# A merged stage of a hybrid encoder layer: backward chunks in two slots and forward chunks in four, in place of one and five

## The chip, the cores and the metric

The kernel runs on one core of one Trainium2 chip, in a single launch. The metric is the device time in microseconds, the median of several runs; less is better. PE is the matmul engine TensorE, DVE is VectorE, ACT is ScalarE, POOL is GpSimd, and SP (SyncE) issues transfers.

## The reference

One encoder layer over two sequences, of 1024 and 2048 tokens (24 chunks of 128 tokens in all), in float32:

```python
h = rms_norm(x, norm_in)
proj = h @ w_in                    # 1024 -> q, k, v, z_attn, z_ssd, xbc, dt_f, dt_b
y_ssd = ssd_branch(...)            # conv, forward and backward chunked scans, gate, norm
y_attn = dilated_mixture(rotary(q), rotary(k), v) * silu(z_attn)
x = x + concat([y_ssd, y_attn]) @ w_out
y = rms_norm(x, norm_f)

def ssd_scan(x, dt_raw, b_mat, c_mat, a_log, dt_bias):   # chunks of 128, 16 heads
    ...
    y_diag = jnp.einsum('bclsge,bcsgep->bclgep', cb[..., None] * lmat, xc)
    states = jnp.einsum('bcsgn,bcsgep->bcgepn', bc, decay_to_end[..., None] * xc)
    # carried from chunk to chunk: carry * chunk_decay + states
    y_off = jnp.einsum('bclgn,bcgepn->bclgep', cc, states_in) * jnp.exp(acum)[..., None]
    return (y_diag + y_off).reshape(bsz, s_len, h, p)
```

The backward scan is the same function on the flipped sequence, so its states are carried from the last chunk of a sequence to the first.

## The kernel before

The kernel runs in phases: a front phase (norm, the first projections, the convolution), two short phases that prepare the decays, the merged stage `late_phase`, the attention, and the output projection. The change touches `late_phase` alone.

`late_phase` does two things side by side. The first is the projection of q, k and za (the attention gate): 144 units from `late_units()`, ordered by turn (three blocks of 1024 tokens), name (q, k, za: 16 units each), pair of weight tiles, half of the block, and ab. A unit is 24 matmuls of 128x128 by 128x512 (L1067): float32 is split into a high and a low part, so that the products are h_hi by w_hi, h_hi by w_lo, h_lo by w_hi, eight of each. The unit's number n is also its slot; u = n % 2 is its output buffer. The second is the scan: for 24 chunks first the backward states (`add_back` on PE, `back_step` on DVE, `weigh` on POOL, `store_back` and `load_back` on SP), and then for 24 chunks the forward pass.

Every engine walks over the slots in the same loop, `for slot, unit in enumerate(units)`: PE does `scan(slot)` and then `multiply(unit)`; DVE does `scan(slot)` and then `rotate(unit)`, if the unit is q or k; ACT does its part of the scan and then `take(unit)`, if the unit is za. The engines are tied together by semaphores, and each engine works strictly in its own order. Slots 0 to 23 carry one backward chunk each (`first_forward = NT`, 24). From slot 24 on a forward chunk has `CYCLE` = 5 slots, its parts:

- part 0: PE computes the diagonal of the chunk before (`diagonal(n - 1)`, 16 heads, L1133) and the first quarter of the decays (`decays`, L1088); DVE `gated(n - 1)` and `choose(n, 0)`; POOL `scale_x` (L907) and `keep_state` (L897); ACT copies the decays and does `norm(n - 1)`.
- part 1: decays, products of B and C (L1100), the forward state's part (`state_part(n, 0)`, L1116); DVE choose, finish, skip_part, state_part.
- part 2: decays, `add_state` (L1124); DVE choose, next_state; POOL `skip_x`.
- part 3: decays, add_state, `state_part(n, 1)`; DVE choose, next_state, state_part; ACT the exponentials (L1191).
- part 4: nothing of the scan on PE; DVE `whole_m(n)` (L1298), which multiplies the 16 decay matrices by C times B; POOL `add_rest(n)` (L922, L925), SP `load_rows(n + 1)` and `load_states(n + 1)`.

`diagonal(n)` waits for `whole_m(n)` (semaphore f_m_steps), for both state parts and for x. `gated(n)` waits for the diagonal and for `add_rest(n)`.

`rotate(unit)` waits for the unit's own products (l_out). For u = 0 it is two instructions (L1240, product with the table). For u = 1 it is two products (L1245) and two additions (L1249, both inputs in SBUF), which turn the pair of units into the rotated rows.

POOL also splits the weights: `split(w)`, two pieces of L871, L874 and a DMA issue (L858), in each slot with slot % 4 = 0 and in each with slot % 4 = 3. It waits there for the last products that use the buffer. The order of POOL's queue in the loop is:

```python
if part == 0: scale_x(n); keep_state(n)
if slot % 4 == 0: split(slot // 2 + 2)
if part == 2: skip_x(n)
if slot % 4 == 3: split(slot // 4 * 2 + 3)
if part == 4: add_rest(n)
```

At the end of a turn ACT loads the next block of h in halves (`load_h`, 2048 KB for h_hi and for h_lo of each half). The first half is issued in the slot after its last use, slots 46 and 94, behind what ACT has of the scan in that slot. `multiply` waits for it at the first unit of the next turn, slots 48 and 96.

Of the kernel before, what the change touches and what calls it, by code (L numbers as in the profile page):

```python
# [32 lines left out]
NT = sum(TILES)  # L33
# [729 lines left out]
    return units  # L763


CYCLE = 5


def late_phase(nc, sem, c, params, scratch, t_in, st, h_hi, h_lo):
# [3 lines left out]

    quads = HEADS // 4
    units = late_units()
    first_forward = NT
    second = TILES[0]
    turned_over = TILES[1]
    weights = len(units) // 2
# [7 lines left out]
    with ExitStack() as stack:  # L787
# [43 lines left out]
        def state_ready(j):  # L831

            return j + 1 + (j >= turned_over)

        def part_of(slot):

# [5 lines left out]
        def _(pool):  # L842
# [87 lines left out]
                split(w)  # L930
            weigh(0)
            for slot in range(len(units)):
                if slot + 1 < first_forward:
                    weigh(slot + 1)
                n, part = part_of(slot)
                if part == 0:
                    scale_x(n)
                    keep_state(n)
                if slot % 4 == 0:
                    split(slot // 2 + 2)  # L940
                if part == 2:
                    skip_x(n)
                if slot % 4 == 3:
                    split(slot // 4 * 2 + 3)
                if part == 4:
                    add_rest(n)

        @block.sync
        def _(sp):
            def load_back(j):  # L950
                if j >= 2:

                    sp.wait_ge(sem["b_added"], j - 1)
                sp.dma_start(xb[:, j % 2, :], by_chunk["xb"][NT - 1 - j, :, :]).then_inc(sem["b_in"][j % 2], 16)

            def store_back(j):
                sp.wait_ge(sem["b_state"], state_ready(j))
                sp.dma_start(scratch["states"][NT - 1 - j, :, :], state[:, j % 2, :]).then_inc(sem["b_stored"][j % 2], 16)

            def load_rows(n):  # L960
                if n:

                    sp.wait_ge(sem["f_seg"], quads * n)
                else:
                    sp.wait_ge(sem["f_rows_set"], 6)
                sums = scratch["sums"].rearrange("(d q h) (c l) -> c d q h l", d=DIR, q=2, l=P)
                for d in range(DIR):
                    at = 64 * d + 2 * HEADS
                    sp.dma_start(rows[at:at + 2, :, :].bitcast(F32), sums[n, d, :, :, :]).then_inc(sem["f_rows_in"], 16)
                sp.dma_start(shift[:, :].bitcast(F32), scratch["shift"][:, n * P:(n + 1) * P]  # L970
                             ).then_inc(sem["f_rows_in"], 16)

            def load_x(n):

                if n < 2:
                    sp.wait_ge(sem["b_added"], NT)
                else:
                    sp.wait_ge(sem["f_diag"], n - 1)
                    sp.wait_ge(sem["f_scaled"], 2 * n - 2)
                sp.dma_start(xb[:, n % 2, :], by_chunk["xb"][n, :, :]).then_inc(sem["f_in"][n % 2], 16)  # L980

            def load_states(n):
                if n:

                    sp.wait_ge(sem["f_off"], 2 * n)
                    sp.wait_ge(sem["f_cb"], n)
                else:
                    for u in range(2):
                        sp.wait_ge(sem["b_stored"][u], 16 * (NT // 2))
                sp.dma_start(bc[:, :, :], scratch["bct"].rearrange("(g n) t -> n g t", n=NST)[:, :, n * P:(n + 1) * P]  # L990
                             ).then_inc(sem["f_states_in"], 16)
                sp.dma_start(s_back[:, :], scratch["states"][n, :, :]).then_inc(sem["f_states_in"], 16)

            def load_gate(n):
                if n:

                    sp.wait_ge(sem["f_out"], n)
                sp.dma_start(gate[:, :], by_chunk["zs"][n, :, :]).then_inc(sem["f_gate_in"], 16)

            def store_y(n):  # L1000
                sp.wait_ge(sem["f_out"], n + 1)
                sp.dma_start(by_chunk["y_ssd"][n, :, :], spare[:, :]).then_inc(sem["f_stored"], 16)

            def store(unit):
                u = unit.u
                sp.wait_ge(sem["l_staged"][u], unit.n // 2 + 1)
                first = unit.b * BLOCK + unit.half * CW
                sp.dma_start(scratch[unit.name][unit.row:unit.row + P, first:first + CW], stage[:, u, :]
                             ).then_inc(sem["l_stored"][u], 16)

            load_back(0)
            load_back(1)
            sp.dma_start(table[:, :, :], t_in["rope"][:, :, BLOCK:]).then_inc(sem["l_rope_in"], 16)
            sp.dma_start(gain[:, :], params["norm_ssd"].to_broadcast([P, D_SSD])).then_inc(sem["f_consts"], 16)
            sp.dma_start(skip[:, :], params["d_skip"].to_broadcast([P, HEADS])).then_inc(sem["f_consts"], 16)
            for slot, unit in enumerate(units):
                if slot < first_forward:
                    store_back(slot)
                    if slot == first_forward - 4:
                        load_rows(0)  # L1020
                        load_gate(0)
                    if slot == first_forward - 1:
                        load_x(0)
                        load_x(1)
                        load_states(0)
                n, part = part_of(slot)
                if part == 1 and n:
                    store_y(n - 1)
                    load_gate(n)
                if part == 4 and n + 1 < NT:  # L1030
                    load_rows(n + 1)
                    load_states(n + 1)
                if part == 1 and 2 <= n + 1 < NT:
                    load_x(n + 1)
                if unit.turn == 1 and unit.name == "q" and unit.n == first_of_half[1, 0]:

                    sp.wait_ge(sem["l_taken"][1], unit.ropes_before // 2)
                    sp.dma_start(table[:, :, :], t_in["rope"][:, :, 0:BLOCK]).then_inc(sem["l_rope_in"], 16)
                if slot + 2 < first_forward:
                    load_back(slot + 2)  # L1040
                if slot:
                    store(units[slot - 1])
            store(units[-1])
            store_y(NT - 1)
            for u in range(2):
                sp.wait_ge(sem["l_stored"][u], 16 * (len(units) // 2))
            sp.wait_ge(sem["f_stored"], 16 * NT)

        @block.tensor
        def _(pe):  # L1050
# [84 lines left out]
                last.then_inc(sem["f_diag"], 1)  # L1135

            def scan(slot):
                if slot < first_forward:
                    add_back(slot)
                n, part = part_of(slot)  # L1140
                if part == 0:
                    if n:
                        diagonal(n - 1)
                    decays(n, 0)
                elif part == 1:
                    decays(n, 1)
                    products(n)
                    state_part(n, 0)
                elif part == 2:
                    decays(n, 2)  # L1150
                    add_state(n, 0)
                elif part == 3:
                    decays(n, 3)
                    add_state(n, 1)
                    state_part(n, 1)
# [73 lines left out]
        def _(dve):  # L1229
# [108 lines left out]
                                               ALU.mult, ALU.mult).then_inc(sem["f_out"], 1)  # L1338

            def scan(slot):  # L1340
                if slot < first_forward:
                    back_step(slot)
                n, part = part_of(slot)
                if part == 0:
                    if n:
# [8 lines left out]
                elif part == 1:  # L1354
                    choose(n, 1)
                    if n:
                        finish(n - 1)
                    skip_part(n)
                    state_part(n, 0)
                elif part == 2:  # L1360
                    choose(n, 2)
                    next_state(n, 0)
                elif part == 3:
                    choose(n, 3)
                    next_state(n, 1)
                    state_part(n, 1)
                elif part == 4:
                    whole_m(n)

            dve.wait_ge(sem["f_consts"], 32)  # L1370
            nc.vector.memset(state[:, 0, :], 0.0).then_inc(sem["b_state"], 1)
            for slot, unit in enumerate(units):
                scan(slot)
                if unit.rope:
                    if unit.turn < 2 and unit.n == first_of_half[unit.turn, 0]:
                        dve.wait_ge(sem["l_rope_in"], 16 * (unit.turn + 1))
                    rotate(unit)
            gated(NT - 1)
            finish(NT - 1)

# [839 lines left out]
```

## Time and profile before

| what | value |
|---|---|
| median of 3 runs | 3931.37 us (3925.37 to 3935.82) |
| the profiled execution | 3925.94 us |
| its span, first to last instruction | 3924.3 us |
| mean granted TensorE clock | 0.957 of full speed |
| PE busy | 3614.0 us (92%) |
| PE weight loads busy | 2850.7 us (73%) |
| DVE busy | 2146.7 us (55%) |
| POOL busy | 1594.6 us (41%) |
| ACT busy | 1360.7 us (35%) |
| POOL's two additions of add_rest, L922 and L925, mean of each | 2.38 and 2.43 us |
| DMA | 521.87 MB, mean 133 GB/s |

Busy times are shares of the whole span, over phases that have different limits. A row of the timeline is a run of equal instructions: when it started, how long it lasted from the first start to the last end, and in brackets how long the engine was idle before it and what released it. "issue" as the releaser says that the profile shows nothing that the engine waited for. The granted clock (PEclk) is 1.00 at 2.4 GHz and 0.50 at 1.2 GHz. Ends of matmuls are modelled; the starts are what periods are taken from.

### The profile page before, as it was taken

How to read it: one execution, taken by the hardware profiler on the slowest of the kernel's cores; microseconds unless marked ns; L12 is line 12 of the kernel's file. 1: busy time of each engine (PE TensorE's matmuls, PEld its weight loads, DVE VectorE, ACT ScalarE, POOL GpSimd, SP SyncE). 2: the span in 40 equal slices, each digit the busy share in tenths (PEclk: the TensorE clock that was granted, in tenths of full speed). 3: DMA queues.
4: the chain of work that ended last, by engine and by line, in shares of the span. 5: the costliest groups of instructions: out<-in, count | busy, mean ns of one | idle time of the engine just before them, and what ended most of it. 6: DMA issues, size and time to landing. Idle time of an engine off the chain costs nothing. (4 is left out here: it accounts for less than half of the span.)

```text
span 3924.3 us, 57718 instructions
## 1 busy us (share of the span) xinstructions
PE 3614.0 (92%) x20917; PEld 2850.7 (73%) x20917; DVE 2146.7 (55%) x4515; ACT 1360.7 (35%) x3566; POOL 1594.6 (41%) x1471
## 2 busy tenths in 40 slices
PE   6899999998875999899989998999999997899998
PEld 5777777887753667677767776677777775788887
DVE  2262145206414664366436653788888887465554
ACT  2122112212110003212322123778778885222222
POOL 5336342453505666567666664424233332100000
PEclk9999999999987999999999999999999998999999
DMA  4424422422314654634453342745544544444443
GB/s 166 150 77 138 170 77 72 136 94 64 102 40 160 212 166 137 209 122 136 128 185 120 122 142 89 172 125 136 137 127 114 139 132 128 162 158 154 166 152 103
DMA packets 366864, 521.87 MB, mean 133 GB/s; under 512 B 27595, under 2 KB 257555, under 8 KB 363859
## 3 DMA queue, kind: packets, MB, share of 16 engines
q1 hardware_dynamic: 329683, 402.80, 32.6%
q0 software_dynamic: 27456, 94.78, 8.1%
q10 hardware_dynamic: 9472, 20.97, 1.5%
q8 instruction: 152, 2.49, 0.3%
q14 instruction: 101, 0.83, 0.1%
HBM read 334.18 MB, written 184.29 MB: 132 GB/s over the span
## 5 line engine op out<-in xcount | busy, mean ns | idle before, releaser
L1713 ACT ACTIVATE attn_p_sb<-attn_p_sb,attn_o_sb 128x256 f32<-128x256 f32 (+1 forms) x1152 | 535.0, 466 | 183.7 <-DVE attn_o_sb L1747 178.2
L235 POOL TENSOR_TENSOR front_w_hi<-front_w_raw,one 128x1024 fp32r<-128x1024 f32 (+1 forms) x96 | 165.9, 1728 | 566.0 <-PE front_out L432 532.2
L1747 DVE CUSTOM_DVE_ANT_0 attn_p_sb<-attn_s_ps,attn_mask 128x256 f32<-128x256 f32 (+1 forms) x1152 | 368.8, 376 | 43.9 <-PE attn_s_ps L1646 43.7
L1067 PE MATMUL late_out<-h_hi,late_w_hi 128*128 128x512 f32 x1152 | 344.5, 443 | 22.5 <-issue 22.5
L1537 POOL COPY attn_q_apart<-attn_q 128x128 f32<-128x128 f32 (+2 forms) x256 | 136.9, 535 | 523.9 <-PE attn_s_ps L1646 517.5
L1067 PEld LDWEIGHTS late_out<-h_hi,late_w_hi 128*128 128x128 f32 x1152 | 225.0, 197 | 119.6 <-issue 78.4
L369 DVE TENSOR_SCALAR front_acc<-front_chan,front_consts 128x1024 f32<-128x1024 f32 (+2 forms) x36 | 38.8, 1077 | 473.3 <-ACT front_chan L281 473.3
L1186 ACT COPY late_m<-late_seg 128x512 f32<-128x512 f32 x96 | 55.9, 583 | 680.4 <-PE late_seg L1088 671.1
L1067 PE MATMUL late_out<-h_hi,late_w_lo 128*128 128x512 f32 x1152 | 286.7, 391 | 0.0
L1067 PE MATMUL late_out<-h_lo,late_w_hi 128*128 128x512 f32 x1152 | 284.5, 389 | 0.0
L1659 PE MATMUL attn_pt_ps<-ident,attn_p_sb 128*128 128x128 f32 x1920 | 278.4, 282 | 0.4 <-ACT attn_p_sb L1713 0.4
L1674 PE MATMUL attn_ot_ps<-attn_pt_sb,attn_v 128*64 128x128 f32 x3840 | 273.2, 280 | 0.0
L1659 PEld LDWEIGHTS attn_pt_ps<-ident,attn_p_sb 128*128 128x128 f32 x1920 | 203.9, 141 | 82.4 <-ACT attn_p_sb L1713 59.3
L375 DVE SCALAR_TENSOR_TENSOR front_acc<-front_chan,front_consts,front_acc 128x1024 f32<-128x1024 f32 (+2 forms) x144 | 258.4, 1795 | 5.1
L1067 PEld LDWEIGHTS late_out<-h_hi,late_w_lo 128*128 128x128 f32 x1152 | 218.4, 190 | 47.0
L432 PE MATMUL front_out<-front_w_hi,h_hi 128*128 128x512 f32 x768 | 203.9, 407 | 51.3 <-POOL front_w_lo L238 35.1
L1067 PEld LDWEIGHTS late_out<-h_lo,late_w_hi 128*128 128x128 f32 x1152 | 216.2, 188 | 45.0
L871 POOL TENSOR_TENSOR late_w_hi<-late_w_raw,one 128x512 fp32r<-128x512 f32 x144 | 152.4, 1058 | 220.1 <-PE late_out L1067 200.5
L1674 PEld LDWEIGHTS attn_ot_ps<-attn_pt_sb,attn_v 128*64 128x64 f32 x3840 | 203.7, 136 | 48.0 <-issue 48.0
L238 POOL TENSOR_TENSOR front_w_lo<-front_w_raw,front_w_hi 128x1024 fp32r<-128x1024 f32 (+1 forms) x96 | 230.1, 2397 | 7.5
L1713 ACT ACTIVATION_READ_ACCUMULATOR attn_p_sb<-attn_p_sb,attn_o_sb 128x1 f32 x1152 | 217.0, 188 | 0.0
L432 PEld LDWEIGHTS front_out<-front_w_hi,h_hi 128*128 128x128 f32 x768 | 147.1, 196 | 86.2 <-POOL front_w_lo L238 39.8
(211 smaller groups left out, 7380.1 us busy)
## 6 DMA issues: line engine op xcount, KB each, us to landing
front_w_raw<-w_in POOLq DMA_DIRECT2D x84, 512.0 KB, 4.1
output_parts<-s_o SPq DMA_DIRECT2D x24, 1584.0 KB, 6.5
late_w_raw<-w_in POOLq DMA_DIRECT2D x144, 256.0 KB, 3.9
s_o<-attn_o_sb SPq DMA_DIRECT2D x128, 264.0 KB, 3.0
late_xb<-s_xb SPq DMA_DIRECT2D x48, 640.0 KB, 5.8
s_zs<-front_stage SPq DMA_DIRECT2D x48, 256.0 KB, 2.0
s_v<-front_stage SPq DMA_DIRECT2D x48, 256.0 KB, 2.2
s_states<-late_state SPq DMA_DIRECT2D x24, 512.0 KB, 3.3
```

What stands on the lines that cost most here:

```text
L235: nc.gpsimd.tensor_tensor(hi, raw, one.to_broadcast([P, 2, cols]), ALU.mult).then_inc(sem["w_split"], 1)
L238: nc.gpsimd.tensor_tensor(lo, raw, hi.bitcast(F32), ALU.subtract).then_inc(sem["w_split"], 1)
L375: nc.vector.scalar_tensor_tensor(a, chan[:, k:k + conv.tokens], consts[:, at:at + 1], a, ALU.mult, ALU.add).then_inc(sem["tap_done" if k < ...
L432: last = nc.tensor.matmul(out[u][:, :], lhs, rhs, start=first, stop=h is h_lo and k == KT - 1)
L871: nc.gpsimd.tensor_tensor(w_hi[w % 3][:, k, :], w_raw[:, piece, :, :], one.to_broadcast([P, KT // 2, P]), ALU.mult).then_inc(sem["l_w_step ...
L1067: last = nc.tensor.matmul(out[u][:, :], w[s][:, k, :], h[:, k, half], start=first, stop=h is h_lo and k == KT - 1)
L1186: nc.scalar.copy(m[:, 4 * q:4 * q + 4, :].rearrange("p h l -> p (h l)"), seg[0][:, :]).then_inc(sem["f_decay"], 1)
L1537: nc.gpsimd.tensor_copy(dst[:, r * n:(r + 1) * n], src[:, at]).then_inc(sem["a_apart"][p - 1], 1)
L1659: last = nc.tensor.transpose(pt_ps[g % 2][:, h, k, :], p_sb[g % 4][:, h, k * P:(k + 1) * P], c["ident"][:, :])
L1674: last = nc.tensor.matmul(ot_ps[cut, g % 2, :], v[step.p][:, pattern.value_chunk(step.i, k), cut], pt_sb[g % 4][:, h, k, :], start=k == 0, ...
L1713: last = nc.scalar.activation(cut, cut, ACT.Exp, scale=-1.0, bias=o_sb[g // 4 % ring][:, g % 4, h, VW:OW], accum_out=o_sb[g // 4 % ring][: ...
L1747: last = nc.vector.tensor_tensor_reduce(out=p_sb[g % 4][:, h, 0:width], in0=s_ps[g % 2][h][:, 0:width], in1=mask[:, step.pattern.strip(ste ...
```

## The change

The backward pass takes 48 slots, a chunk in each even one. A forward chunk takes four slots, so that the forward pass begins at slot 48 and ends with slot 143 as before. What was in part 4 moves to part 3: `add_rest` on POOL, `load_rows` and `load_states` on SP, and `whole_m` on DVE, where it stands behind `rotate` of the same slot.

```diff
-CYCLE = 5
+CYCLE = 4
...
-    first_forward = NT
+    first_forward = 2 * NT
...
+        def chunk_back(slot):
+
+            return slot // 2 if slot < first_forward and slot % 2 == 0 else None
+
...  (POOL)
-                if slot + 1 < first_forward:
-                    weigh(slot + 1)
+                j = chunk_back(slot)
+                if j is not None and j + 1 < NT:
+                    weigh(j + 1)
...
-                if part == 4:
+                if part == 3:
                     add_rest(n)
...  (SP)
+                j = chunk_back(slot)
                 if slot < first_forward:
-                    store_back(slot)
+                    if j is not None:
+                        store_back(j)
...
-                if part == 4 and n + 1 < NT:
+                if part == 3 and n + 1 < NT:
                     load_rows(n + 1)
                     load_states(n + 1)
...
-                if slot + 2 < first_forward:
-                    load_back(slot + 2)
+                if j is not None and j + 2 < NT:
+                    load_back(j + 2)
...  (PE)
-                if slot < first_forward:
-                    add_back(slot)
+                if chunk_back(slot) is not None:
+                    add_back(chunk_back(slot))
...  (DVE)
-                if slot < first_forward:
-                    back_step(slot)
+                if chunk_back(slot) is not None:
+                    back_step(chunk_back(slot))
...
-                elif part == 4:
-                    whole_m(n)
...
                     rotate(unit)
+                n, part = part_of(slot)
+                if part == 3:
+                    whole_m(n)
```

## Rows read from the trace of the kernel before

**Rows 1.** The page, part 1: busy time, share of the span and instructions.

```profile
PE 3614.0 (92%) x20917; PEld 2850.7 (73%) x20917; DVE 2146.7 (55%) x4515; ACT 1360.7 (35%) x3566; POOL 1594.6 (41%) x1471
```

**Rows 2.** Busy time by stretch, with granted clock, DMA share, GB/s.

```profile
1230.27:1424.08 193.81, 181.12 (x673) 128.63 (x674) 131.08 (x116) 0.00 (x0) 132.49 (x96) 0.96 0.64 207
1424.08:2433.57 1009.49, 963.28 (x4195) 725.82 (x4195) 533.16 (x627) 264.45 (x337) 631.21 (x466) 0.96 0.42 139
```

**Rows 3.** Timeline of PE, backward slots 3, 4 and 5 (their first rows).

```profile
1253.81 1.88 PE L1076 MATMUL late_work<-late_scaled,late_xb 128*128 128x512 f32 x4
...
1261.01 1.88 PE L1076 MATMUL late_work<-late_scaled,late_xb 128*128 128x512 f32 x4
...
1270.89 3.06 PE L1076 MATMUL late_work<-late_scaled,late_xb 128*128 128x512 f32 x4 [2.51 <-DVE late_state L1262]
```

**Rows 4.** Timeline of PE, first rows of slots 54 to 59 (chunk 6, then diagonal).

```profile
1674.97 3.68 PE L1133 MATMUL late_work<-late_xb,late_m 128*128 128x64 f32 x32
...
1684.67 0.50 PE L1088 MATMUL late_seg<-late_rows,late_shift 64*128 64x512 f32 x2
...
1692.92 0.50 PE L1088 MATMUL late_seg<-late_rows,late_shift 64*128 64x512 f32 x2
...
1699.86 0.50 PE L1088 MATMUL late_seg<-late_rows,late_shift 64*128 64x512 f32 x2
...
1708.44 1.98 PE L1067 MATMUL late_out<-h_hi,late_w_hi 128*128 128x512 f32 x8
...
1716.44 4.96 PE L1133 MATMUL late_work<-late_xb,late_m 128*128 128x64 f32 x32 [2.40 <-issue]
```

**Rows 5.** Timeline of chunk 2, whose units are za: DVE and PE, slots 37 to 39.

```profile
1534.86 2.35 DVE L1298 TENSOR_TENSOR late_m<-late_m,late_cb_ps 128x1024 f32<-128x1024 f32 x2
...
1538.98 1.98 PE L1067 MATMUL late_out<-h_hi,late_w_hi 128*128 128x512 f32 x8
...
1544.42 3.68 PE L1133 MATMUL late_work<-late_xb,late_m 128*128 128x64 f32 x32
```

**Rows 6.** Timeline of PE and the DMA issues of ACT at the two h loads.

```profile
1627.89 3.75 PE L1067 MATMUL late_out<-h_hi,late_w_hi 128*128 128x512 f32 x8 [10.31 <-issue]
...
2013.82 0.53 ACTq L1173 DMA_DIRECT2D h_hi<-s_h  x1
...
2036.39 3.56 PE L1067 MATMUL late_out<-h_hi,late_w_hi 128*128 128x512 f32 x8 [12.14 <-issue]
```

**Rows 7.** Waits, 1430 to 2440 us: in total, times, longest us.

```profile
PE late_work L1133 <- issue: 18.1, 8, 2.4
```

**Rows 8.** Timeline of DVE and POOL behind the part 3 products of chunk 6.

```profile
1708.64 1.29 DVE L1245 TENSOR_TENSOR late_stage<-late_out,late_table 128x512 f32<-128x512 f32 x2 [4.24 <-PE late_out L1067]
...
1709.31 1.91 POOL L907 TENSOR_TENSOR late_scaled<-late_xb,st_weight 128x1024 f32<-128x1024 f32 x1
...
1709.96 4.11 DVE L1249 TENSOR_TENSOR late_stage<-late_a_turned,late_stage 128x512 f32<-128x512 f32 x2
...
1714.00 2.34 DVE L1298 TENSOR_TENSOR late_m<-late_m,late_cb_ps 128x1024 f32<-128x1024 f32 x2
```

**Rows 9.** Timeline of DVE, whole_m of chunk 5, whose part 3 is even.

```profile
1670.93 2.34 DVE L1298 TENSOR_TENSOR late_m<-late_m,late_cb_ps 128x1024 f32<-128x1024 f32 x2
```

**Rows 10.** Timeline of DVE, the longest pair of L1249, slot 64.

```profile
1760.14 6.04 DVE L1249 TENSOR_TENSOR late_stage<-late_a_turned,late_stage 128x512 f32<-128x512 f32 x2
```

**Rows 11.** Timeline of POOL, the split of slot 27 (1445.40), first and last row.

```profile
1445.55 1.04 POOL L871 TENSOR_TENSOR late_w_hi<-late_w_raw,one 128x512 fp32r<-128x512 f32 x1 [5.60 <-PE late_out L1067]
...
1451.77 0.79 POOL L858 DMA_DIRECT2D late_w_raw<-w_in  x1 [0.29 <-DMA late_w_raw<-w_in]
```

**Rows 12.** Busy time and granted clock in the diagonal of slot 99.

```profile
2060.11:2067.10 6.99, 6.99 (x33) 6.87 (x34) 1.09 (x2) 0.00 (x0) 3.98 (x5) 0.50 0.57 187
```

**Rows 13.** Timeline of PE, first rows of slots 99 and 100.

```profile
2060.11 7.06 PE L1133 MATMUL late_work<-late_xb,late_m 128*128 128x64 f32 x32 [2.40 <-issue]
...
2074.64 0.50 PE L1088 MATMUL late_seg<-late_rows,late_shift 64*128 64x512 f32 x2
```

## The prediction

> **What bounds the kernel now.** I read the page first: TensorE (PE) is busy 92% of the span [rows 1]. Then the stretches. The merged stage runs from the first backward product at 1230.27 to the last projection product at 2433.57, 1203.3 us: 193.81 us for the 24 slots that carry the backward chunks, 1009.49 us for the 120 slots of the forward chunks [rows 2]. PE works almost without a break in both, and the change gives it the same matmuls in another order. So I price only what PE loses: each slot's period, from its first matmul to the next slot's, against the shortest period of its kind.
>
> PE's rows in order of time give these shortest periods. A slot with a backward chunk takes 7.20 us (1253.81 to 1261.01) [rows 3]. Of a forward chunk, part 0 (the diagonal of the chunk before, then decays) takes 9.70, part 1 8.25, part 2 6.94, part 3 8.58 [rows 4], and part 4, which carries the projection alone, 5.44 (1538.98 to 1544.42) [rows 5]. A chunk is 38.91. Chunk 0 has no diagonal ahead of it, 3.61 us less.
>
> - Backward: 193.8 - 24 x 7.2 = 21 us lost. Every fourth slot ends with PE waiting 2.5 us for VectorE's state update (1261.01 to 1270.89 is 9.88, not 7.20) [rows 3]: five such waits at 2.7 are 13.4 us, and the slow restarts after some of them about 5. The other 2 are the start of the stage and stay.
> - Forward: 1009.5 - (24 x 38.9 - 3.6) = 79 us lost. 26 of it lies at the two places where h is replaced: PE idles 10.31 and 12.14 us, and the restarts run slow (8 matmuls in 3.75 and 3.56 us) [rows 6]. The other 53 lie around eight waits of the diagonal, L1133, 18.1 us of gap in all [rows 7], their slow restarts, and a few waits of 0.5 to 1.4 us for a late choose.
>
> **What the eight waits are.** The diagonal needs whole_m (L1298). At the end of chunk 6, part 3 has an odd slot, so `rotate` of that slot has four instructions, and they wait for its products, which end at 1708.44. VectorE then runs L1245 (1708.64), the pair L1249 from 1709.96 for 4.11 us, and only then whole_m, 1714.00 to 1716.34 [rows 8]. The diagonal starts at 1716.44, 8.0 us after the products of part 3; part 4 covers 5.44 of them [rows 4]. In the chunk before, part 3 is an even slot: whole_m runs 1670.93 to 1673.27 and the diagonal at 1674.97 does not wait [rows 9]. Where the units are gates (za) VectorE has no rotate: whole_m ends at 1537.2, 1.8 us before the end of the part 3 products at 1538.98 [rows 5].
>
> **The change part by part.**
>
> 1. Backward chunk in two slots (48 slots, 24 with a chunk). Per two slots PE has 7.2 + 5.4 = 12.6 us, and VectorE one state step and one pair of rotates instead of two steps. I take the waits for the state as gone: 21 - 2 = -19 us. POOL's weigh is half as frequent too. If the cover failed it would be the 2.5 us wait again, so at most 0.
>
> 2. The forward waits go in their old form: -53 us. They belong to a pattern (whole_m in part 4, odd and even slots in turn) that is no longer there; what comes in its place is the next point.
>
> 3. Part 4 removed, whole_m after `rotate` of part 3. Forward chunks now start at slot 48, so part 3 is slot 51 + 4n: always odd, u = 1. The diagonal is the first thing that PE does in the next slot. No slot lies between, so the whole distance "end of the part 3 products to end of whole_m" becomes idle time of PE. It applies where the part 3 slot is q or k: slots 48 to 79 and 96 to 127, 16 chunks. For the 8 chunks in za slots it costs 0 by [rows 5] (cover 1.8 us).
>  - Size of the wait. L1245 begins 0.2 after the products; the pair L1249 begins 1.5 after them. How long the pair takes is the unknown: at least 1.29 us, what the pair L1245 of the same shape takes, 4.11 beside POOL's L907 [rows 8], 6.04 at worst [rows 10]. Which one? The split of a weight runs in slots 4k+3, which is now always part 3: from 1445.55 to 1452.56, 7.0 us [rows 11], beginning with the slot. add_rest (L922 and L925, 2.4 each by the table of the profile) is behind it: it runs 7.2 to 12.0 us after the start of part 3, and the products end at 8.58. So when the pair comes, at 10.1, POOL is in L925, then in L907. Let the first half of the pair wait for the end of L925 (12.0, done 12.7) and the second for L907 (14.4, done 15.0): 4.9 us. With whole_m at 2.34 the diagonal starts 17.4 after the start of part 3, a wait of 8.8. Bounds: 0.2 + 1.3 + 1.3 + 2.3 + 0.1 = 5.2, and with the pair at 6.04, 9.9.
>  - Clock. After PE's wait of 2.4 us at 2060.11 the granted clock is 0.50 for the 6.99 us of the diagonal (1.2 of 2.4 GHz), and the slot lasts 2074.64 - 2060.11 = 14.53 instead of 9.70: 4.8 us [rows 12, 13]. The new wait is over three times as long, so I take this, the dearest common case. Low bound: the restart at 1627.89 without a diagonal, 16 matmuls in 6.7 us instead of 4.0, 2.7 us [rows 6]. High bound, an estimate: the slow stretch of [rows 12] and the same again on all of the projection products, 6.
>  - Behind the waiting diagonal in PE's queue stand the decays of the next chunk and the products of part 0; nothing passes it, so the time is lost. VectorE's gated and choose of part 0 come later by the same amount as PE's part 1, which needs them, and POOL's scale_x and keep_state run meanwhile: no second wait.
>  - 16 x (8.8 + 4.8) = +218 us.
>
>  The pair's 4.9 us rests on the two engines excluding each other. In the trace the first L1249 of [rows 8] stands beside L907 and takes 4.11 us where L1245's pair takes 1.29. The Trainium skill, SBUF — State Buffer, "Who interferes with whom", says that a VectorE instruction with two SBUF inputs contends with a GpSimd instruction that reads SBUF, the later one blocking fully. By that rule the pair is 4.9 and the wait 8.8; without it 1.29 and 5.2. The trace agrees in size.
>
> 4. Replacing h. The first replacement now has slots 46 and 47 as backward slots in front of it, 7.2 + 5.4 + 0.4 of cover instead of 6.94 + 8.58: +2.5. At the second, slots 94 and 95 become parts 2 and 3, and slot 96 begins with a diagonal. The load was issued at 2013.82 in ScalarE's queue, 9 us into the slot, behind norm [rows 6]; in part 2 it has no norm in front of it and goes out about 8 us earlier. Landing some 25 us after, against 19.6 of cover: about -6. Together -4. SyncE's waits move with their parts: load_rows and load_states now stand in part 3, where f_off is released 2.7 us into the slot, and the next q store behind them has to wait for a rotate anyway. The rows are needed after the diagonal, more than 12 us later. 0.
>
> Sum: -19 - 53 + 218 - 4 = +142 us. The profiled execution took 3925.9 (span 3924.3 and 1.6 around it): 4068. The median of the runs is 5.4 above it, so 4073.
>
> **The rivals.**
>
> - A, the pair is short (POOL has passed by): 16 x (5.2 + 4.8) = 160, total +84, 4015. Against: POOL's split starts with part 3 by its own wait, so add_rest meets the pair in each chunk.
> - B, the clock costs less. The restart at 2036.39, dense projection products, lost 3.56 - 2.40 = 1.2 us [rows 6], the one at 1627.89 2.7. With 2.7: 16 x 11.5 = 184, +108, 4039. Against: each restart here begins with the diagonal of 64-column products, as in [rows 12, 13]. The Trainium skill, TensorE: Matmul & The Clock Gate, "What's actually happening", sees the ramp penalty below 1% of a typical span. That is 39 us; the sum would be 16 x 8.8 + 39 - 76 = +104, 4035. The trace speaks against it where PE waits at each chunk.
> - C, dearer: pair at 6.04 and the clock at 6 us: 16 x 15.9 = 254, +178, 4109; the same if za chunks begin to wait because ScalarE's exp comes 2 us later.
> - D, faster: whole_m ends within the products of part 3, as in [rows 9], for q and k too. Then nothing is added: -76, 3855. It decides below 76 / 16 = 4.8 us lost per chunk. The lower bound of the wait alone is 5.2, as rotate cannot start before the products end and stands in front. Only if VectorE's order were other than I read it.
>
> **How the numbers follow.** Forecast 0.60, A 0.12, B 0.14, C 0.11, D 0.03. The time is that of the forecast, 4073. The range 4012 to 4110 reaches from A to C. All cases but D are slower by far over 0.3% (12 us, about what a measurement of this kernel can tell from no change): slower 0.96, faster 0.03, same 0.01.
>
> **What would show it.** In the changed kernel's trace: L1133 with 16 gaps of about 9 us put down to "issue", none in za slots; a granted clock near 0.5 behind each; L1249 at 4 to 6 us in slots 4k+3 with POOL's L925 and L907 beside it; no wait for L1262 in the backward slots. The stage would last some 1345 us. Wrong would be: waits at za chunks, gaps of 5 us, or a diagonal at full clock.

## The result and the profile after

The changed kernel took 4074.9 us (median of 4 runs, 4074.4 to 4076.3) against 3929.0 us before (3925.4 to 3935.8): a ratio of 1.0367, 95% interval 1.0354 to 1.0379. It is 146 us slower. The forecast was 4073.

In the changed kernel the line numbers have moved: L1083 is the backward product (before L1076), L1074 the projection (L1067), L1140 the diagonal (L1133), L1252 and L1256 the two pairs of rotate (L1245, L1249), L1305 whole_m (L1298), L926, L929, L911, L901 POOL's add_rest, scale_x and keep_state (L922, L925, L907, L897), L1180 the load of h (L1173).

Busy time by stretch, backward slots and then forward slots (engines in the order PE, PEld, DVE, ACT, POOL, then granted clock, DMA share, GB/s). It answers to [rows 2]:

```profile
1230.75:1536.19 305.44, 305.44 (x1248) 234.97 (x1248) 170.03 (x145) 10.25 (x16) 204.11 (x166) 0.99 0.57 181
1536.19:2580.78 1044.59, 896.12 (x3620) 672.10 (x3619) 491.00 (x598) 247.68 (x315) 552.66 (x396) 0.86 0.37 120
```

PE is busy for all of the backward stretch, at a mean granted clock of 0.99. In the forward stretch it is busy for 896 of 1045 us, and the mean granted clock fell from 0.96 to 0.86. The stage lasts 1350.0 us against 1203.3.

The timeline of PE in two backward slots and the one after, which answers to [rows 3]:

```profile
1257.88 1.88 PE L1083 MATMUL late_work<-late_scaled,late_xb 128*128 128x512 f32 x4
...
1265.09 1.98 PE L1074 MATMUL late_out<-h_hi,late_w_hi 128*128 128x512 f32 x8
...
1270.53 1.88 PE L1083 MATMUL late_work<-late_scaled,late_xb 128*128 128x512 f32 x4
```

A slot with a chunk takes 7.21 us and one without 5.44, and no slot ends in a wait for the state: the 21 us above the shortest periods shrank to 2.1, nearly all of it in the first slot.

The waits of the forward stretch (total us, times, longest), which answer to [rows 7]:

```profile
PE late_work L1140 <- issue: 133.1, 16, 8.5
```

One of the 16, at slot 76. The timeline of PE, beside [rows 4, 13]:

```profile
1857.11 0.50 PE L1095 MATMUL late_seg<-late_rows,late_shift 64*128 64x512 f32 x2
...
1863.87 1.97 PE L1074 MATMUL late_out<-h_lo,late_w_hi 128*128 128x512 f32 x8
1874.31 7.06 PE L1140 MATMUL late_work<-late_xb,late_m 128*128 128x64 f32 x32 [8.46 <-issue]
1881.30 0.80 PE L1095 MATMUL late_seg<-late_rows,late_shift 64*128 64x512 f32 x2
...
1889.65 0.50 PE L1095 MATMUL late_seg<-late_rows,late_shift 64*128 64x512 f32 x2
```

Part 3 lasts 1874.31 - 1857.11 = 17.20 us instead of 8.58, and the next part 0 15.34 instead of 9.70. What VectorE and POOL do meanwhile, in their timelines, beside [rows 8]:

```profile
1865.88 1.29 DVE L1252 TENSOR_TENSOR late_stage<-late_out,late_table 128x512 f32<-128x512 f32 x2 [4.24 <-PE late_out L1074]
1867.21 4.74 DVE L1256 TENSOR_TENSOR late_stage<-late_a_turned,late_stage 128x512 f32<-128x512 f32 x2
1871.87 2.34 DVE L1305 TENSOR_TENSOR late_m<-late_m,late_cb_ps 128x1024 f32<-128x1024 f32 x2
...
1866.75 2.34 POOL L929 TENSOR_TENSOR late_y<-late_y,late_spare 128x1024 f32<-128x1024 f32 x1
1869.05 2.35 POOL L911 TENSOR_TENSOR late_scaled<-late_xb,st_weight 128x1024 f32<-128x1024 f32 x1
```

The chain reads without a gap: products end (1865.70, the start of the slot plus the shortest period of a part 3, 8.58), L1252, the pair L1256, whole_m to 1874.21, the diagonal at 1874.31. The first of the pair stands behind L929 and the second behind L911, which is what the prediction laid out. VectorE had been idle for 4.24 us ahead of L1252.

The clock in the same place, busy time by stretch (the wait, the diagonal, decays and the first eight products, the rest of the slot), beside [rows 12]:

```profile
1865.70:1874.31 8.61, 0.15 (x2) 0.03 (x1) 8.29 (x6) 0.00 (x0) 8.53 (x5) 0.70 0.20 77
1874.31:1881.30 6.99, 6.99 (x32) 6.87 (x32) 0.00 (x0) 0.00 (x0) 5.56 (x6) 0.50 0.14 38
1881.30:1885.60 4.30, 4.30 (x11) 3.10 (x11) 3.09 (x3) 2.17 (x4) 0.00 (x0) 0.50 0.23 61
1885.60:1889.65 4.05, 4.05 (x17) 3.07 (x15) 0.00 (x0) 2.63 (x4) 0.00 (x0) 0.92 0.02 4
```

The clock is 1.2 GHz for all of the diagonal, for the decays and for the first third of the products behind it. In none of the 16 slots does PE have a gap behind the start of the diagonal, so what such a slot loses is lost to the clock alone. For comparison the 4.30 us behind the diagonal of [rows 12], in the kernel before:

```profile
2067.10:2071.40 4.30, 4.30 (x14) 3.17 (x14) 3.09 (x3) 2.18 (x4) 0.00 (x0) 0.63 0.00 0
```

The loads of h, timelines of PE and of ScalarE's DMA issues, beside [rows 6]:

```profile
1549.17 3.75 PE L1074 MATMUL late_out<-h_hi,late_w_hi 128*128 128x512 f32 x8 [12.47 <-issue]
...
2046.66 0.54 ACTq L1180 DMA_DIRECT2D h_hi<-s_h  x1
...
2068.66 3.75 PE L1074 MATMUL late_out<-h_hi,late_w_hi 128*128 128x512 f32 x8 [2.92 <-issue]
```

The first wait grew from 10.31 to 12.47 us; the second fell from 12.14 to 2.92.

The difference, taken as each slot's period above the shortest period of its kind:

| where | before | after | difference |
|---|---|---|---|
| backward slots | 21.0 | 2.1 | -18.9 |
| first load of h | 13.2 | 15.3 | +2.1 |
| second load of h | 13.9 | 5.5 | -8.4 |
| wait for whole_m (end of the chunk's last slot) | 19.5 | 135.5 | +116.0 |
| part 0: slow restarts, and before also late chooses | 32.1 | 88.3 | +56.2 |
| other slots | 0.5 | 0.1 | -0.4 |
| sum | 100.2 | 246.8 | +146.6 |

The table is made from the two profiled executions. They took 4074.5 and 3925.9 us, 148.6 apart, so it accounts for all but 2.0 us; these lie outside the stage, and nothing here shows where. The medians differ by 146.0.

### The profile page after: what moved, and what is told of

Its sections match the earlier page's. It is cut to its first block and busy times, and to the rows that moved or that the text cites. A ratio compares the mean times of both kernels' runs of the same rounds, so it can differ in the third digit from the quotient of the medians.

```text
span 4072.6 us, 57712 instructions
## 1 busy us (share of the span) xinstructions
PE 3672.9 (90%) x20917; PEld 2903.6 (71%) x20917; DVE 2144.3 (53%) x4515; ACT 1354.1 (33%) x3560; POOL 1589.6 (39%) x1471
## 5 line engine op out<-in xcount | busy, mean ns | idle before, releaser
L1074 PE MATMUL late_out<-h_hi,late_w_hi 128*128 128x512 f32 x1152 | 357.5, 456 | 15.4 <-issue 15.4
L1074 PEld LDWEIGHTS late_out<-h_hi,late_w_hi 128*128 128x128 f32 x1152 | 233.5, 205 | 114.7 <-issue 70.9
L1074 PE MATMUL late_out<-h_hi,late_w_lo 128*128 128x512 f32 x1152 | 291.3, 396 | 0.0
L1074 PE MATMUL late_out<-h_lo,late_w_hi 128*128 128x512 f32 x1152 | 284.6, 389 | 0.0
L1140 PE MATMUL late_work<-late_xb,late_m 128*128 128x64 f32 x768 | 142.4, 372 | 133.1 <-issue 133.1
L1074 PEld LDWEIGHTS late_out<-h_hi,late_w_lo 128*128 128x128 f32 x1152 | 223.0, 194 | 49.1
L1074 PEld LDWEIGHTS late_out<-h_lo,late_w_hi 128*128 128x128 f32 x1152 | 216.3, 188 | 45.2
L1140 PEld LDWEIGHTS late_work<-late_xb,late_m 128*128 128x128 f32 x768 | 140.2, 285 | 140.0 <-issue 139.4
```

Source lines behind the costliest of these rows:

```text
L1074: last = nc.tensor.matmul(out[u][:, :], w[s][:, k, :], h[:, k, half], start=first, stop=h is h_lo and k == KT - 1)
L1140: last = nc.tensor.matmul(work[:, h * DH:(h + 1) * DH], m[:, h, :], xb[:, n % 2, h * DH:(h + 1) * DH], start=True, stop=True)
```

## The experiments

Each ran beside the kernel before on the same chip. The medians of the kernel before were 3936.8 us in the first group (the first four) and 3935.3 in the second, 6 to 8 us above the 3929.0 of the main comparison, so the ratios count.

**1. whole_m ahead of rotate, in the changed kernel.**

```diff
                 elif part == 3:
                     choose(n, 3)
                     next_state(n, 1)
                     state_part(n, 1)
+                    whole_m(n)
...
                     rotate(unit)
-                n, part = part_of(slot)
-                if part == 3:
-                    whole_m(n)
```

> The changed kernel with one edit: whole_m stands in part 3 behind state_part, ahead of rotate. Theory (whole_m behind rotate makes PE wait for the whole distance): whole_m then runs some 5 to 7.5 us into part 3, the products end at 8.6, and the 16 waits of the diagonal and their slow restarts go. From the changed kernel's 4075: minus 16 x (8.5 + 5.4) = -222, so about 3853 us, below both kernels. Rival (the pattern of four slots itself is too tight for VectorE, whatever the place of whole_m): waits of several us stay at the diagonal or at the decays, and the time is above 3929.

Measured: 3853.8 us, ratio to before 0.9795 (0.9776 to 0.9815); from the 3929.0 of the main comparison that ratio gives 3848. The timelines of VectorE and PE in slot 67 (part 3 starts at 1708.54):

```profile
1713.00 2.34 DVE L1305 TENSOR_TENSOR late_m<-late_m,late_cb_ps 128x1024 f32<-128x1024 f32 x2
1717.35 1.29 DVE L1252 TENSOR_TENSOR late_stage<-late_out,late_table 128x512 f32<-128x512 f32 x2 [2.01 <-PE late_out L1074]
1718.67 4.72 DVE L1256 TENSOR_TENSOR late_stage<-late_a_turned,late_stage 128x512 f32<-128x512 f32 x2
...
1717.15 3.68 PE L1140 MATMUL late_work<-late_xb,late_m 128*128 128x64 f32 x32
```

whole_m fills what was VectorE's idle time under the products, and ends at 1715.34, 1.8 us before they do. The diagonal follows at once at full clock. The pair L1256 takes 4.72 us as before; nobody on PE waits for it. By the same count as in the table, 0.1 us is left of the 135.5 and 2.0 of the 88.3. The rival falls. This kernel is faster than both the kernel before and the changed one.

**2. The same move in the kernel before, with its slots as they are.**

```diff
                     state_part(n, 1)
-                elif part == 4:
                     whole_m(n)
```

> The kernel before with one edit: whole_m moves from part 4 to the end of part 3's scan work, ahead of rotate. Slots are divided as before (one and five). Theory: the eight waits of the diagonal with their slow restarts go, and most of the 53 us around them: about 3929 - 50 = 3880 us. What then remains between this kernel and the changed one with the same place of whole_m is the backward part, 19 us, and the loads of h, a few us. Rival (the eight waits come from POOL's add_rest or from the state parts, not from rotate ahead of whole_m): they stay, 3929 us.

Measured: 3886.8 us, ratio 0.9881 (0.9863 to 0.9899), -50 us on this chip; from the 3929.0 of the main comparison that ratio gives 3882. The end of each chunk lost 0.0 us instead of 19.5, part 0 lost 9.9 instead of 32.1, all of it for late chooses. The backward slots kept their 20.9 us and the loads of h their 26.8. Against experiment 1 it is 33 us slower; by the count of the traces that is 18.9 backward, 7.2 at the loads of h, 7.9 for late chooses.

**3. POOL's add_rest only after the additions of rotate.**

```diff
                 if part == 3:
+                    if units[slot].rope:
+                        pool.wait_ge(sem["l_staged"][1], slot // 2 + 1)
                     add_rest(n)
```

> The changed kernel with one edit: in the 16 chunks whose part 3 slot is q or k, POOL begins add_rest only when the additions of rotate (L1249 of the kernel before) are done. Theory (the pair of additions is held up by POOL's L925 and L907): the pair falls from nearly 5 us to 1.3, the wait of the diagonal from 8.6 to about 5.2 us, 16 x 3.4 = -54 us or a little less, since the clock stays low behind a wait of 5 us as well: about 4021 us. Rival (the pair takes that long by itself or for its operands): no change, 4075 us, or slower because add_rest is late for gated.

Measured: 4024.6 us, ratio 1.0231 (1.0212 to 1.0250), that is 53 us below the changed kernel by the two ratios. The timelines of VectorE and POOL behind the products of slot 59:

```profile
1672.45 1.29 DVE L1254 TENSOR_TENSOR late_stage<-late_out,late_table 128x512 f32<-128x512 f32 x2 [4.24 <-PE late_out L1076]
1673.77 1.29 DVE L1258 TENSOR_TENSOR late_stage<-late_a_turned,late_stage 128x512 f32<-128x512 f32 x2
1674.98 2.35 DVE L1307 TENSOR_TENSOR late_m<-late_m,late_cb_ps 128x1024 f32<-128x1024 f32 x2
...
1675.15 2.34 POOL L926 TENSOR_TENSOR late_spare<-late_spare,late_scaled 128x1024 f32<-128x1024 f32 x1 [4.32 <-DVE late_stage L1258]
```

With POOL quiet the same pair takes 1.29 us instead of 4.74, and the wait is 5.2 us in all 16 places (82.7 in sum): the lower bound of the prediction to the tenth. whole_m, beside POOL's L926, keeps its 2.35. The cost of the clock was 91.8 us where it was 88.3: behind a wait of 5.2 us the restart cost as much as behind one of 8.6. The rival falls.

**4 and 6. Unused products in PE's wait.** 32 of them in experiment 4, 38 in experiment 6:

```diff
                     if n:
+                        if units[slot - 1].rope:
+                            pe.wait_ge(sem["f_added_used"], 2 * n)
+                            for k in range(32):
+                                nc.tensor.matmul(added[:, :], h_hi[:, 0, 0:P], h_hi[:, k % KT, 0:CW],
+                                                 start=True, stop=True)
                         diagonal(n - 1)
```

> The changed kernel with 32 extra products of 128x128 by 128x512 on PE ahead of the diagonal in the 16 chunks where it waits; their result goes to a free PSUM buffer and is not used. They take some 7.2 us of the 8.6 us wait. Theory (PE's idle time lowers the clock, and the slow restart costs 5.4 us per wait): the diagonal runs at 2.4 GHz in 3.6 us instead of 7.0, 16 x 5.4 = -87 us, about 3988 us, with the waits' ends where they were. Rival (the diagonal after such a wait is slow for another reason, or the extra products delay it): 4075 us or more.

Measured: 4017.9 us, ratio 1.0213 (1.0195 to 1.0231). It gained 61 us by the ratios where 87 were expected. The timeline of PE at slot 60 shows what was left:

```profile
1667.42 7.41 PE L1153 MATMUL late_added<-h_hi 128*128 128x512 f32 x32
1676.10 5.82 PE L1140 MATMUL late_work<-late_xb,late_m 128*128 128x64 f32 x32 [1.27 <-issue]
```

Behind a gap of 1.27 us the diagonal takes 5.8 us, not 3.7: it begins fast and the clock falls on its way. This is the dearest of the 16 places. The same gap eight slots later did nothing:

```profile
1759.94 7.41 PE L1153 MATMUL late_added<-h_hi 128*128 128x512 f32 x32
1768.63 3.76 PE L1140 MATMUL late_work<-late_xb,late_m 128*128 128x64 f32 x32 [1.27 <-issue]
```

The gap was 1.26 to 1.30 us in 14 places and 0.11 in two. The clock fell in seven of the 14, where the slot lost 3.1 to 4.7 us more than in the others, 25 us in sum, about what is missing from the 87. In the other nine places the diagonal took 3.76 us. Experiment 6 closes the gap. Its expectation says that the clock fell in most of the 16 places; by this count it was seven.

> As the kernel with the filler products, but 38 of them in place of 32, which fill the 8.6 us wait to its end. With 32 a gap of about 1.2 us was left, the diagonal began at 2.4 GHz and in most of the 16 places fell to 1.2 GHz on its way; the cost of the clock was about 30 us in place of 88. Theory (any gap ahead of the sparse diagonal is enough for the fall): without the gap the diagonal stays at 3.6 us, and the time is 4075 - 88 = 3987 us, or a few us more where the filler overruns the wait. Rival (the 64-column products of the diagonal lower the clock by themselves after a wait of VectorE's length): as with 32, 4018 us or more.

Measured: 3990.9 us, ratio 1.0141 (1.0124 to 1.0158), 89 us below the changed kernel by the ratios. The same slot:

```profile
1667.83 8.78 PE L1153 MATMUL late_added<-h_hi 128*128 128x512 f32 x38
1676.54 3.76 PE L1140 MATMUL late_work<-late_xb,late_m 128*128 128x64 f32 x32
```

The diagonal takes 3.68 to 3.76 us in all 16 places. It still begins 8.6 to 8.7 us after the end of the useful products, and nothing useful is done in that time, yet nearly all of the clock's 88 us are gone: in the trace the slots of part 0 lose 140.5 us, about 5 more than the waits of 135.5. So the two costs, the wait and the restart, are separate and both real, and the 64-column products of the diagonal do not lower the clock by themselves where no idle time stands in front of them.

**5. Part 3 on even slots.**

```diff
-    first_forward = 2 * NT
+    first_forward = 2 * NT - 1
...
-            if slot < first_forward:
+            if slot < first_forward or slot >= first_forward + CYCLE * NT:
                 return None, None
```

> The changed kernel with the forward part one slot earlier (it begins at slot 47, slot 143 carries no scan), so that part 3 falls on even slots; whole_m stays behind rotate. Rotate of an even slot is two instructions (1.3 us) in place of four. Theory: the wait of the diagonal is 0.2 + 1.3 + 2.3 = 3.9 us instead of 8.6, the slow restart 4.8 to 5.4; 16 x 5 = -80 us from the changed kernel's 4075, about 3995 us, still slower than before. Rival (whole_m is late for the exponentials on ScalarE, not for rotate): the waits stay near 8 us, 4075 us.

Measured: 3997.9 us, ratio 1.0151 (1.0134 to 1.0168), 85 us below the changed kernel by the ratios. The timelines of VectorE and PE at slots 58 and 59 (the products of part 3 end at 1656.94):

```profile
1657.16 1.29 DVE L1247 TENSOR_TENSOR late_a_turned<-late_out,late_table 128x512 f32<-128x512 f32 x2 [3.74 <-PE late_out L1074]
1658.37 2.34 DVE L1305 TENSOR_TENSOR late_m<-late_m,late_cb_ps 128x1024 f32<-128x1024 f32 x2
...
1660.81 7.06 PE L1140 MATMUL late_work<-late_xb,late_m 128*128 128x64 f32 x32 [3.69 <-issue]
```

The wait is 3.87 us, the length of an even rotate and whole_m. The clock cost 84.3 us over the 16 places, hardly less than the 88.3 behind waits twice as long. The exponentials had no part in these 16 waits. They had one in a seventeenth, in slot 130, whose unit is za (the other seven za slots of part 3 had none), where `whole_m` began behind the exponentials on ScalarE (L1198) and the diagonal waited as well:

```profile
2395.30 2.35 DVE L1305 TENSOR_TENSOR late_m<-late_m,late_cb_ps 128x1024 f32<-128x1024 f32 x2 [0.78 <-ACT late_m L1198]
...
2397.75 4.94 PE L1140 MATMUL late_work<-late_xb,late_m 128*128 128x64 f32 x32 [1.15 <-issue]
```

It cost 4.6 us with its restart. The edit also moves POOL's split out of part 3, since that stays at slot % 4 = 3; the 16 waits are the sum of rotate and `whole_m` all the same.

**7. The load of h at the head of ScalarE's slot, in the kernel before.**

```diff
             for slot, unit in enumerate(units):
+                if unit.n + 1 < len(units) and unit.turn < 2:
+                    for half in range(2):
+                        if unit.n == last_of_half[unit.turn, half] + 1:
+                            load_h(unit.turn + 1, half)
                 n, part = part_of(slot)
                 if part == 0:
...
                     exponentials(n)
-                if unit.n + 1 < len(units) and unit.turn < 2:
-                    for half in range(2):
-                        if unit.n == last_of_half[unit.turn, half] + 1:
-                            load_h(unit.turn + 1, half)
```

> The kernel before with one edit: in ScalarE's order the load of the next h stands at the head of the slot, ahead of copy_decays and norm. Theory: the second load (slot 94, part 0) goes out 8 to 9 us earlier, and PE's wait of 12.1 us at slot 96 falls to 4 to 6 us; the first (slot 46, part 2) goes out 0.6 us earlier at most and its wait of 10.3 stays. About -7 us: 3922 us; the trace shows it more surely than the time. Rival (the transfer is bound by the DMA queues' other traffic, not by its issue): both waits stay.

Measured: 3918.7 us, ratio 0.9956 (0.9939 to 0.9973). The load went out at 2007.14 in a slot that starts at 2006.94, and PE had no wait at slot 96 at all, where 4 to 6 us were expected. One came two slots later, for the second half of h:

```profile
2045.25 3.63 PE L1067 MATMUL late_out<-h_hi,late_w_hi 128*128 128x512 f32 x8 [4.68 <-DMA h_lo<-s_h]
```

By the count of the table the two loads lost 19.4 us instead of 27.1, close to the 7 expected, and the stage as a whole 90.1 instead of 100.1; the rest of the 10 lies in the diagonal's waits, of which seven were left of eight, and their restarts. The medians differ by 17, with an interval of 11 to 24, and nothing here shows where the part beyond 10 comes from. The rival falls for the second load, and the first (9.85 us of wait) stayed as expected. So the issue time set the second load's wait. In the changed kernel the load went out 0.55 us into its slot (2046.66, the slot starts at 2046.11) instead of 9.1, while the distance from that slot's start to the products of slot 96 that need it stayed (19.5 us before, 19.6 after); this is where the -8.4 us there come from.

## Why the prediction was right

1. Backward chunk in two slots: -19 forecast, -18.9 found. Experiments 1 and 2 differ by it once more.
2. The old forward waits: -53 forecast, -52 found (19.5 + 32.1 + 0.5). Experiment 2 shows that rotate ahead of whole_m caused the eight waits.
3. The new wait: 16 x 8.8 = 141 forecast, 135.5 found, 8.6 in 14 chunks and 7.4 in two (slots 55 and 115). The prediction's chain was POOL's L925 until 12.0 us into the slot, then L907 until 14.4; in slot 76's chain they end at 12.0 and 14.3. In slot 55 POOL's last DMA issue of the split came 0.8 us late, so that the pair L1256 met POOL's additions one step earlier and took 3.56 us. Of the rivals, A is what experiment 3 made, 5.2 us (priced 4015, by the ratio 4020); the prediction's choice between 1.29 and 4.9 for the pair was the term that mattered, and POOL's order in the slot decided it. The Trainium skill, SBUF — State Buffer, "Who interferes with whom", has a VectorE instruction with two SBUF inputs contend with POOL's reads, and one with a single SBUF input not. Experiment 3 agrees with both: L1256 is held up by POOL (4.74 against 1.29 us), and whole_m, one input of which is in PSUM, takes 2.35 beside L926.
4. The clock: 16 x 4.8 = 77 forecast, 88 found, 5.5 each. The term was taken from the slot after a wait of 2.4 us [rows 13]; there part 0 took 14.53 us in all, here 15.34 at slot 76, because the clock came back later. In the 4.30 us behind the diagonal it was 0.63 at slot 99 of the kernel before and 0.50 at slot 76. Taking 4.8 was a choice, and a right one: of the eight waits of the kernel before, four cost 4.8 us of clock, two 3.2 and two nothing (see the last section). That the new wait is over three times as long was the reason given, and in all 16 places the cost was 4.7 to 6.1. The low bound of 2.7, from a restart without a diagonal, was not approached in any of them, so rival B falls by the changed kernel's own trace, and experiment 6 shows that it is PE's idle time that costs this. The figure of the Trainium skill, TensorE: Matmul & The Clock Gate, "What's actually happening" (a ramp penalty below 1% of a typical span), taken for all 16 restarts together, would have made at most 39 us of it, an estimate. The trace does not agree: measured are 88, and the measurement decides.
5. The loads of h: -4 forecast, -6.3 found; the second was sized at -6 and gave -8.4. The prediction let the load land 25 us after its issue and named no row for that. In [rows 6] PE goes on 22.6 us after the issue, in the changed kernel 22.0.
6. D, the faster rival, needed VectorE's order to be other than read. Experiment 1 is that order, and gave 3854 (3848 by the ratio) where D was priced at 3855. Of C, the pair never took 6 us and no slot with a za unit waited in the changed kernel; experiment 5 shows one such wait.

The mechanism was right in each part. That the total came so close is partly luck: the two errors in size, 141 for 135.5 and 77 for 88, had opposite signs, and the change was forecast at +142 and measured at +146, while the median that it was added to, 3931.4, lay 2.4 us above the one measured beside the changed kernel.

## What to carry to other kernels

When stages are merged slot by slot, look at what each engine does between "the products end" and "what the next slot's first instruction needs": work that does not need this slot's products has to stand ahead of the work that does. Removing a slot in which the bound engine has nothing of the scan to do also removes the cover of whatever was late behind it; here 5.44 us of cover went, and the same instructions in another order (experiment 1) turned +3.7% into -2.1%. TensorE's wait ahead of the diagonal cost its length and a slow restart, and the restart can be the larger part (5.3 against 3.9 us in experiment 5).

## What the runs showed of the hardware beyond that

- Behind waits of 3.9 us and more the restart was slow in all 48 places, and its cost hardly depended on the length of the wait: 5.3, 5.7 and 5.5 us in the mean behind waits of 3.9, 5.2 and 8.6 us (experiments 5, 3 and the changed kernel), with 4.7 to 6.2 us as the range of single places.
- Behind shorter gaps it went either way. Of the 14 gaps of 1.3 us in experiment 4, the clock fell within the diagonal behind seven and stayed up behind seven. Of the eight gaps of 2.1 to 2.4 us in the kernel before it fell behind six: with a gap of 2.40 us the diagonal took 4.96 us once [rows 4] and 7.06 once [rows 13], and with 2.14 us the one of slot 69, shown below, ran at full speed. What decides between the two is not shown.
- Without a gap the clock never fell: not in the 16 diagonals of the kernel before that follow the products at once, and not in the 16 places of experiment 6.

```profile
1801.30 3.76 PE L1133 MATMUL late_work<-late_xb,late_m 128*128 128x64 f32 x32 [2.14 <-issue]
```

What a short wait costs must therefore be read over all its places; one row of a trace does not tell it.
